# Two transformer blocks on one core: hardware loops written out, the final norm folded, operand addresses moved, tables kept in SBUF, gate columns merged

## The reference, cut to what matters

```python
def first_block(x, ...):                 # 2 layers, then a final norm
    for l in range(2):
        x = x + 0.5 * swiglu(rmsnorm(x, g_ffn1[l]), w1_a[l], w3_a[l], w2_a[l])      # width 2816
        p = rmsnorm(x, g_mix[l]) @ w_in[l]            # Fourier, pooling, short convolution, three gates
        x = x + merged @ w_o[l]
        x = x + 0.5 * swiglu(rmsnorm(x, g_ffn2[l]), w1_b[l], w3_b[l], w2_b[l])
    return rmsnorm(x, g_final)
def second_block(x, ...):                # 2 layers
    for l in range(2):
        x = x + 0.5 * swiglu_2(rmsnorm_2(x, ffn1_norm[l]), ...)
        z = rmsnorm_2(x, mix_norm[l]) @ w_in[l]
        q_a, k_a, v_a, q_b, k_b, v_b, r_b, g_lr, gate_a, gate_b = split_cols(z, IN_SPLITS)
        # window attention on q_a, k_a, v_a; gated linear attention on q_b, k_b, v_b with
        log_a = log_sigmoid(g_lr @ gla_w_gate[l] + gla_gate_bias[l]) / 16     # g_lr: 16 columns
        x = x + merged @ w_out[l]
        x = x + 0.5 * swiglu_2(rmsnorm_2(x, ffn2_norm[l]), ...)
```

## Time and profile before

| | |
|---|---|
| median of 3 runs | 2428.81 us (2428.69 to 2429.35) |
| the profiled execution's own time | 2430.38 us |
| its span, first to last instruction | 2428.4 us |
| PE busy | 2378.7 us, 98% of the span, 10966 matmuls |
| DVE, ACT busy | 1339.0 us (55%), 1184.1 us (49%) |
| DMA engines, mean of the span | 173 GB/s |
| granted TensorE clock, mean | 0.993 |

### The profile page before, as it was taken

How to read it: one execution, slowest core, us unless ns; L and a number is a source line. 1 busy time by engine, 2 the same in 40 slices (tenths; PEclk the granted TensorE clock), 3 DMA queues, 4 the chain that set the end, 5 groups by cost and what they waited for, 6 DMA issues and landing times.

```text
span 2428.4 us, 31240 instructions
## 1 busy us (share of the span) xinstructions
PE 2378.7 (98%) x10966; PEld 1941.7 (80%) x10966; DVE 1339.0 (55%) x1470; ACT 1184.1 (49%) x1270; POOL 0.2 (0%) x4
## 2 busy tenths in 40 slices
PE   7999999999999999998999999999999999999999
PEld 6887887887887787887788878788878887878887
DVE  4554566555555456554555566755455447576554
ACT  5444444545544344544544565455455446545543
POOL 0000000000000000000000000000000000000000
PEclk9999999999999999999999999999999999999999
DMA  6656355555556455665465542555555554335653
GB/s 193 191 181 219 131 192 181 189 186 173 179 185 216 142 170 173 190 191 181 143 189 193 179 156 87 157 170 177 194 171 181 191 193 161 100 124 172 190 178 134
DMA packets 311170, 419.14 MB, mean 173 GB/s; under 512 B 16990, under 2 KB 202086, under 8 KB 311048
## 3 DMA queue, kind: packets, MB, share of 16 engines
q1 hardware_dynamic: 306496, 409.13, 52.3%
q10 hardware_dynamic: 4552, 8.47, 1.0%
HBM read 416.50 MB, written 1.05 MB: 172 GB/s over the span
## 4 chain that ended last, share of the span: by engine, by line
PE 89%; DVE 3%; DMA 3%; ACT 2%; issue 2%; SPq 0%; ACTq 0%; DVEq 0%
PE psum L496 27%; PE psum L498 27%; PE psum L497 27%; PE psum L513 3%; DMA raw<-w_in_dram 1%; PE psum L745 1%; ACT whi L979 1%; DVE wlo L1402 1%; PE psum L758 1%; PE psum L586 1%; DMA raw<-w_conv_out_dram 0%; DMA raw<-w_b_dram 0%; PE psum L736 0%; PE psum L603 0%; SPq L375 0%
## 5 line engine op out<-in xcount | busy, mean ns | idle before, releaser
L1402 DVE TENSOR_TENSOR wlo<-raw,whi 128x2048 fp32r<-128x2048 f32 (+2 forms) x410 | 893.2, 2188 | 610.9 <-ACT whi L979 602.8
L979 ACT ACTIVATE whi<-raw 128x2048 fp32r<-128x2048 f32 (+2 forms) x411 | 748.6, 1832 | 515.3 <-DMA raw<-w_in_dram 106.8
L496 PE MATMUL psum<-whi,xt_hi 128*128 128x512 f32 (+1 forms) x2176 | 865.5, 398 | 9.4 <-DVEq L1431 5.9
L498 PE MATMUL psum<-whi,xt_lo 128*128 128x512 f32 (+1 forms) x2176 | 846.4, 389 | 0.0
L497 PE MATMUL psum<-wlo,xt_hi 128*128 128x512 f32 (+1 forms) x2176 | 844.6, 388 | 0.0
L496 PEld LDWEIGHTS psum<-whi,xt_hi 128*128 128x128 f32 x2176 | 412.4, 190 | 95.6 <-issue 17.6
L498 PEld LDWEIGHTS psum<-whi,xt_lo 128*128 128x128 f32 x2176 | 411.9, 189 | 85.6
L497 PEld LDWEIGHTS psum<-wlo,xt_hi 128*128 128x128 f32 x2176 | 412.9, 190 | 81.5 <-issue 2.9
L496 PE MATMUL psum<-whi,ht_hi 128*128 128x512 f32 x704 | 279.7, 397 | 0.0
L497 PE MATMUL psum<-wlo,ht_hi 128*128 128x512 f32 x704 | 278.3, 395 | 0.0
L498 PE MATMUL psum<-whi,ht_lo 128*128 128x512 f32 x704 | 278.2, 395 | 0.0
(11 more groups left out here) (225 smaller groups left out, 1474.3 us busy)
## 6 DMA issues: line engine op xcount, KB each, us to landing
raw<-w_in_dram SPq DMA_DIRECT2D x180, 512.0 KB, 4.5
raw<-w_a_dram SPq DMA_DIRECT2D x128, 512.0 KB, 4.8
raw<-w_b_dram SPq DMA_DIRECT2D x128, 512.0 KB, 4.8
raw<-ffn_w_gate_dram SPq DMA_DIRECT2D x88, 512.0 KB, 4.1
raw<-ffn_w_up_dram SPq DMA_DIRECT2D x88, 512.0 KB, 5.1
raw<-ffn_w_down_dram SPq DMA_DIRECT2D x80, 512.0 KB, 4.7
raw<-w_o_dram SPq DMA_DIRECT2D x16, 512.0 KB, 4.6
raw<-w_proj_b_dram SPq DMA_DIRECT2D x16, 512.0 KB, 4.7
```

Source lines behind the costliest of these rows:

```text
L496: nc.tensor.matmul(pair(p, m)[:, out], hi[:, c, t], whi[:, slot, w], start=first, stop=False)
L498: last = nc.tensor.matmul(pair(p, m)[:, out], lo[:, c, t], whi[:, slot, w], start=False, stop=final)
L979: nc.scalar.activation(whi[:, u % HL, 0:n], raw[:, u % RAW, 0:n], ACT.Copy).then_inc(hi_done, 1)
L1402: nc.vector.tensor_tensor(wlo[:, u % HL, 0:n], raw[:, u % RAW, 0:n], whi[:, u % HL, 0:n], ALU.subtract).then_inc(w_ready, 1)
```

## The change

- Loops are written out in Python: `layers` and `turns` are plain `for` loops, and waits are on constants.
- Between the blocks, the transposed x takes the product of `g_final` and the first `ffn1_norm` as its gain (`V_FOLDED`), unnormalised. The final norm's factor `rfin` and the next norm's `rstd` are computed in `stage_start` of block 2's first FFN (`final_norm`), and their product scales the gates and `hid`. x itself is multiplied there.
- A tensor `spacer` and the moved tables put every tensor after the small vectors at a multiple of 128 bytes (`ht_hi` at 130688).
- `poolm`, `cs`, `cc` stay for both layers of block 1, `spans`, `pairs`, `window`, `rope` for both of block 2. SP issues all tables. `RAW` is 3.
- Units u0+2 and u0+3 of block 2's mixer hold k, v and gate columns together (272 columns, 4 chunks each).
- `loga` is split into `loga_hi` and `loga_lo`, `spans` is float32r, and an exponent is two float32r matmuls.
- At the start the transposed x (`t_xt`) and the gain vectors (`t_vecs`) come from the host's layout as inputs, and unit 0 is loaded and split in halves.
- ACT's order: unit u0+4 is split after `tok` and no longer before it. In block 2's mixer `gl` follows `kv`, and `glt` comes ahead of the root. The transposes of x for the second FFN stand one quarter later.
- At the end of the last FFN there are no transposes, and the halves of x are stored as they are ready.

```diff
-RAW = 2
+SPACER = 56
+RAW = 3
...
     def turns(self, n):
-        with self.eng.Fori(0, n) as self.it:
-            yield
-        self.it = None
+        for self.it in range(n):
+            yield self.it
+        self.it = 0
...
+        sb(ctx, "spacer", [P, SPACER])
+        tables2 = ExitStack()
+        spans = sb(tables2, "spans", [P, 3, 512], F32R)
...
                     for m in range(MT):
                         out = bank(("ex", h, part, m))
-                        nc.tensor.matmul(out, loga[:, m, h * DK:(h + 1) * DK], spans[:, part and 1 + m, :],
-                                         start=True, stop=True).then_inc(small, e.mark(small, ("ex", h, part, m)))
+                        d = slice(h * DK, (h + 1) * DK)
+                        nc.tensor.matmul(out, loga_hi[:, m, d], spans[:, part and 1 + m, :], start=True, stop=False)
+                        nc.tensor.matmul(out, loga_lo[:, m, d], spans[:, part and 1 + m, :],
+                                         start=False, stop=True).then_inc(small, e.mark(small, ("ex", h, part, m)))
...
-                blocks(u0 + 2, 0, 1, XT, range(8), True, True, True, 256)
-                blocks(u0 + 3, 0, 2, XT, range(8), True, True, True, RANK)
+                blocks(u0 + 2, 0, 1, XT, range(4), True, False, True, KV_GLR)
+                blocks(u0 + 3, 0, 1, XT, range(4, 8), False, True, True, KV_GLR)
...
-                wide(u, 1, MERGED, 0, 1)
+                wide(u, 1, MERGED, 0, 2)
                 eng.wait_ge(done, e.after(done, ("x", "ffn1", 0)))
                 x_transposes("ffn1", 0)
-                wide(u, 1, MERGED, 1, 4)
+                wide(u, 1, MERGED, 2, 4)
...
-            eng.wait_ge(consts_in, 16 * N_CONSTS)
-            for b in (1, 2):
-                nc.tensor.transpose(psum[:, 3 + b, 0:VR[b]], vrows[0:VR[b], b - 1, :],
-                                    ident[0:VR[b], 0:VR[b]]).then_inc(small, e.mark(small, ("vecs", b)))
-            x_transposes("ffn0", 0)
+            eng.wait_ge(first_ready, 1)
+            eng.wait_ge(done, e.after(done, ("xt", "ffn0", 0, 0)))
+            blocks(0, 0, 0, XT, (0, 1), True, False, False, ready=False)
...
+                if stage == "ffn0" and (e.block, e.lay) == (2, 0):
+                    squares("final", out)
+                    root("final")
+                    split(u0 + 3)
+                    eng.wait_ge(done, e.after(done, ("x2",)))
+                    squares(stage, out)
+                    root(stage)
...
+            def final_norm(u0):
+
+                norm("final", rfin)
+                split(u0 + 3)
+                eng.wait_ge(gfin_in, 16)
+                for m in range(MT):
+                    ins = nc.vector.scalar_tensor_tensor(out=x[:, m, :], in0=x[:, m, :], scalar=rfin[:, m:m + 1],
+                                                         in1=gfin[:, :], op0=ALU.mult, op1=ALU.mult)
+                ins.then_inc(done, e.mark(done, ("x2",)))
+                norm("ffn0", rstd)
+                ins = nc.vector.tensor_tensor(rstd[:, :], rstd[:, :], rfin[:, :], ALU.mult)
...
+                    e.link(nc.vector.tensor_copy(loga_hi[:, m, :], part))
+                    nc.vector.tensor_tensor(loga_lo[:, m, :], part, loga_hi[:, m, :], ALU.subtract).then_inc(
+                        done, e.mark(done, ("loga_lo", m)))
```

More of the change, by code:

```diff
@@ L91, in __init__ @@
         self.eng, self.counts, self.known, self.own = eng, counts, known, own
[L92 to L101, removed]
+        self.block, self.lay, self.it, self.raised = "start", 0, 0, {}
     def mark(self, semaphore, label):
@@ L115, in after, with start @@
             return 1
[L116 to L124, removed]
+        return self.known.labels[(self.counts.names[id(semaphore)], self.block, self.lay, label)]
+    def start(self, semaphore, label):
+        if self.known is None:
+            return 1
+        return self.known.labels[(self.counts.names[id(semaphore)], "start", 0, label)]
     def link(self, ins):
@@ L479, in pair, with blocks @@
                 return psum[:, 2 * p + m, :]
-            def blocks(u, block, p, split, chunks, start, stop, used, cols=512, beside=False):
+            def blocks(u, block, p, split, chunks, start, stop, used, cols=512, beside=False, ready=True):
                 hi, lo = split
                 slot = u % HL
-                if block == 0:
+                if block == 0 and ready:
                     eng.wait_ge(w_ready, units(e, u, RAW))
@@ L959, in _ @@
                 ffn_tensor(FFN_UNITS + MIX_UNITS[1], 1, "ffn0")
-            e.enter("between")
-            eng.wait_ge(done, e.after(done, ("final", 0)))
-            x_transposes("ffn0", 0)
-            with e.layers(2):
+            for _ in e.layers(2):
                 ffn_tensor(0, 0, "mix")
                 mix2_tensor(FFN_UNITS)
-                ffn_tensor(FFN_UNITS + MIX_UNITS[2], 1, "ffn0")
-            e.enter("end")
+                ffn_tensor(FFN_UNITS + MIX_UNITS[2], 1, "ffn0" if e.lay + 1 < LAYERS else "end")
         @block.scalar
@@ L1468, in stage_start @@
                 split(u0 + 2)
-                x_lo(stage, 1)
-                norm(stage)
-                split(u0 + 3)
+                if e.unit(u0) > 0:
+                    x_lo(stage, 1)
+                if stage == "ffn0" and (e.block, e.lay) == (2, 0):
+                    final_norm(u0)
+                else:
+                    norm(stage, rstd)
+                    split(u0 + 3)
                 if stage == "mix":
@@ L1524, in ffn_vector @@
                     add_to_x(1, 1, 0.5).then_inc(x_whole, 1)
+                if next_stage == "end":
+                    multiplied(u0 + FFN_UNITS - 1)
+                    for m in range(MT):
+                        part = x[:, m, 512:D]
+                        nc.vector.scalar_tensor_tensor(out=part, in0=psum[:, 2 + m, :], scalar=0.5, in1=part,
+                                                       op0=ALU.mult, op1=ALU.add).then_inc(out_ready, 1)
             def mix1_vector(u0):
```

512 lines of the change are left out of this document (302 added, 210 removed).

## The result

The changed kernel takes 2351.2 us (median of 4 runs, 2351.0 to 2352.1) against 2429.1 of the kernel before beside it: ratio 0.9676, 95% interval 0.9659 to 0.9693, or 3.2% faster. The profiled span is 2349.4 us, 79.0 less than the 2428.4 of before; the mean granted clock is 0.999.

A forecast was written before the change was run, and what follows sets the result against it. The prediction took PE, 89% of the chain that ended last, to bound the kernel. Its terms summed to 77.7 us off the profiled 2430.4, and less 1.6 to the median gave 2351 us, range 2341 to 2369.

The forecast's parts named there:

- 1 addresses: FFNs and mixers: 2880 matmuls speed up by 6 ns once their stationary operands lie at multiples of 128 bytes; 17.3 us.
- 2 exponents: Block 2's mixer: 16 float32 calls of 1.72 us become float32r calls of 0.91; 13 us, range 10 to 14.
- 3 gate columns: Block 2's mixer: merged k, v and gate columns shorten PE's work and keep the clock up; 15 us, range 10 to 17.
- 4 between the blocks: Last `ht` matmul to transposes of `hid`: 31.7 us shrinks to a 22.5 chain plus 1.3 for the clock; gain 8.
- 4 transposes dropped: Two stages lose transposes that the following stage doesn't need; 1.7 us.
- 5 loops: Ends of hardware loops in both blocks: PE's gap, mostly "issue", goes when loops are written out; 2.9 us.
- 6 block 1's mixer: PE's waits for `tok`, `merged` and x shrink through ACT's order, tables and third `raw` slot; 10 us, range 6 to 12.
- 7 start: Kernel start: half of x and unit 0 suffices, first matmul at about 8.8; gain 8.8 us, range 6 to 10.
- 8 end: Kernel end: halves of x are stored earlier; 1 us, range 0 to 3.
- The addresses: Rival: moving operands to multiples of 128 gives nothing, 2368 us; chance 0.12.
- no chain came late: Rival denied here: PE waits for the rotary embedding or doubled norm chain, with half clocks; 2362 us, chance 0.17.
- written-out code: Rival: about 77 more instruction packets arrive late, each stopping PE 1.44 us; 2462 us, chance 0.03.

The follow-up runs named there:

- e2: Changed kernel with a spacer 8 floats longer, all stage tensors 32 bytes past a multiple of 128: 2367.5 us.
- e3: Changed kernel with a spacer 16 floats longer, all stage tensors 64 bytes past a multiple of 128: 2367.1 us.
- e1: Kernel before plus one unused 32-byte tensor behind `nt`, so later tensors lie at multiples of 128 bytes: 2412.3 us.
- e5: Changed kernel with the float32 exponents of before, without DVE's cast and subtraction for `loga`: 2361.0 us.
- e6: Changed kernel with k and v columns and the 16 gate columns apart again, as before: 2369.3 us.
- e4: Changed kernel with only the streamed weights displaced to 32 bytes past a multiple of 128: 2409.9 us.
- e11: Changed kernel with streamed weights and all stationary operands displaced alike, 32 bytes past a multiple of 128: 2351.9 us.
- e7: Changed kernel with ACT's split of unit u0+4 put back ahead of `tok` in block 1's mixer: 2351.3 us.
- e8: Changed kernel with the transposes of x for the second FFN one quarter earlier again, in both blocks' mixers: 2351.1 us.
- e12: Changed kernel with two raw slots, the u0+4 split ahead of `tok` and the earlier transposes of x, all put back together: 2354.2 us.
- e9: Changed kernel with two slots of `raw` again, addresses still at multiples of 128: 2353.2 us.

## Why the prediction was right, and where it was not

Forecast 2351 against 2351.2 measured. By terms:

| term | forecast | measured | from |
|---|---|---|---|
| 1 addresses | 17.3 | 16 to 17 | e2, e3; e1 with 1.7 off for the clock |
| 2 exponents | 13 | 9.8 | e5 |
| 3 gate columns | 15 | 16.7 | e6, spans (18.1 by medians) |
| 4 between the blocks | 8 | 9.1 | 31.7 - 20.9, less 3.41 / 2 for the clock |
| 4 transposes dropped | 1.7 | 1.7 | 16 fewer in the trace, eight take 0.87 |
| 5 loops | 2.9 | 3.1 | gaps gone from the trace, 1.66 and 1.44 |
| 6 block 1's mixer | 10 | 12.6 | traces |
| 7 start | 8.8 | 7.7 | 37.16 - 29.43 |
| 8 end | 1 | 1.2 | traces |

The column sums to 78, against 79.0 between the two spans. So the total is not right by chance of one large term, but the errors of terms 2, 3, 4, 6 and 7 do cancel (-3.2, +1.7, +1.1, +2.6, -1.1): that the forecast met the measured time to 0.2 us is luck.

Term 6 is measured from the first `xt` matmul behind an FFN to the first of the next FFN. In the second layer that is 769.78 to 957.41 before, 187.63 us, and 750.13 to 928.05 after, 177.92; in the first 182.74 and 177.96. Of the 14.5 in sum, 288 matmuls by 6.5 ns, 1.9, belong to term 1. Of the 12.6 that are left, 9.0 are waits of PE that are gone in these two stretches, and 1.7 is the half clock behind the second wait for `tok` (3.41 us from 786.77). Term 8 is the time from the last matmul's start to the end of the span, 6.06 before and 4.86 after.

**Term 1** had the right size by a wrong rule. "`ht` lies at 32 past a multiple of 64 and is slow" fitted all rows before, because the weights lay at multiples of 128 throughout; e4 and e11 show that the pair counts. By the rule as I put it, weights displaced as in e4 would have cost nothing; they cost 59 us.

**Term 2** was mis-sized. It took 16 calls at full difference. The step that failed is "other waits in this stretch may come to the surface", which I put into the range and not into the sum: before, a float32 call also covered PE's wait for ACT's `xg`, and that wait is what shows now, 1.6 of the missing 3.2.

**Term 3** held, and the stall on `qkr` that I subtracted (0.7 per layer) did not come, by a margin of 0.4 us. With two slots it came, once.

**Term 4.** The chain was 20.9 long and not 22.5: the steps behind the second root, from 1132.5 to 1135.4, took 2.9 and not the 4 that I allowed, since silu's table load on ACT and the factor on DVE ran side by side. The stand and the half clock after it were as forecast in kind (3.3 us and 3.41 at 0.50, against 4.9 and 1.3 lost).

**Term 6** failed in its reasons: "the first is what the later split of u0+4 takes away, and the third what the moved transposes of x do". Neither edit does anything alone (e7, e8), and both with two slots don't bring `tok`'s wait back (e12). I had looked at what ACT did ahead of `tok` and not at why that unit's DMA was late. Nothing in the traces speaks against my sentence that "Moving table loads to SP's queue costs nothing", but the tables are where the gain for `tok` most likely came from. That sentence also gave the third slot the part of their cover; it is worth 2.0 us by the medians (e9). Why the wait of 2.5 for `merged` went, no run shows: it came back in none of e7 to e12.

**Term 7.** PE's first matmul came at 10.02 and not at 8.8; from there to `hid` it was 19.4, near the forecast 19.6. The step that was off is how early half of x and half of unit 0 are there. With half a split (0.95) and DVE's half (1.2), 8.8 left ACT's first split to begin at 6.6; it began at 7.67:

```profile
7.67 1.04 ACT L1468 ACTIVATE whi<-raw 128x1024 fp32r<-128x1024 f32 x1
```

The first half of unit 0 had landed at 7.35, and until 7.67 ACT was at the transposed x.

**Rivals.** The addresses gave what was forecast; no chain came late; and written-out code did not slow PE: PE's waits list none for it. The step of that rival that was wrong is the number of packets. It counted one of two queues and took fetching to grow with the length of the code; both together moved 122 packets before and 120 after.

## What to carry to other kernels

Where the pace of one matmul shape differs between operands, displace each operand alone and then both together before giving the address a rule. Where an engine stands for a DMA with an urgent operation queued behind, look at when that DMA was issued, how long it took and what else was transferring, before changing the order. Behind a small result that a long chain needs (a factor), put the chain's next step first, and the weights' work under the waits that follow: one line moved gave 4.7 us here.

## What was not expected of the hardware

- In these runs a float32r matmul of 512 columns starts 0.227 us after its forerunner when the two operands' addresses are alike modulo 128 bytes, and 0.232 to 0.234 when they are not, by 32, 64 or 96 bytes. Displacing both by 32 bytes (e11) is as fast as displacing neither.
- With 256 columns it is the other way round. The matmuls with `fq` and `pl` come some 117 ns apart in the kernel before and 119 in the changed kernel. In e1, which moved addresses alone, it is 119 too, so the addresses decide here as well; why in this direction stays open. Twelve with `fq` take 1.40 us before and 1.43 in e1, first before, then e1:

```profile
292.26 0.28 PE L496 MATMUL psum<-whi,fq_hi 128*128 128x256 f32 x1
...
293.66 0.40 PE L496 MATMUL psum<-whi,xt_hi 128*128 128x512 f32 x1
```

```profile
290.02 0.28 PE L497 MATMUL psum<-whi,fq_hi 128*128 128x256 f32 x1
...
291.45 0.40 PE L497 MATMUL psum<-whi,xt_hi 128*128 128x512 f32 x1
```

- PE can be busy without a gap and still lose the clock: it fell to 0.50 among the 48 matmuls of 16 columns, for 6.83 us in each layer of e6, as before, and was 1.00 with the columns merged.
- Writing the loops out hardly changed what was fetched: the two instruction queues moved 1.54 MB before and 1.69 after.
